# Pointwise convolution of six blocks as three products of rounded parts, in a one-core streaming encoder layer

## What is computed

```python
u = cv * jax.nn.sigmoid(cgl)
c = depthwise_conv(concat([conv_hist, u]), conv_w) + conv_b      # 31 taps, 256 channels
c = jax.nn.silu(layernorm(c, ln_g, ln_b)) @ w_pw + b_pw          # pointwise: 256 x 256
y_conv = c * jax.nn.silu(cg)
y = concat([y_attn, y_gla, y_conv]) @ w_out
return x + y
```

## Time and profile before

| | us |
|---|---|
| median of 3 runs | 925.39 (924.95 to 925.93) |
| the profiled execution, its own time | 925.71 |
| its span in the trace | 923.9 |
| PE busy | 890.1 (96%) |
| DVE busy | 784.4 (85%) |
| ACT busy | 481.6 (52%) |
| POOL busy | 215.7 (23%) |

### The profile page before, as it was taken

The page is one execution under the profiler, slowest core; times in us unless marked ns, Lnnn a source line. Parts: engine busy times, 40 slices in busy tenths (PEclk is TensorE's granted clock), DMA queues, the critical chain, the costliest instruction groups (busy, mean ns, idle before and its releaser), DMA issues. The chain is left out here.

```text
span 923.9 us, 15888 instructions
## 1 busy us (share of the span) xinstructions
PE 890.1 (96%) x5655; PEld 800.9 (87%) x5655; DVE 784.4 (85%) x1896; ACT 481.6 (52%) x1182; POOL 215.7 (23%) x259
## 2 busy tenths in 40 slices
PE   6889999999999999998999999999999999999997
PEld 5778888888888888876898888889999899998985
DVE  7898888888888888889879999888788969788994
ACT  7787666666676766668663261341515124142231
POOL 1432222222222222223022231311202012120310
PEclk9999999999999999999999999999999999999999
DMA  9553323222333333135451221121130312204021
GB/s 303 190 191 115 103 82 115 96 110 84 111 106 111 114 115 103 70 120 145 119 160 52 76 69 64 52 81 57 38 101 1 100 39 69 70 3 135 1 81 60
DMA packets 58062, 88.04 MB, mean 95 GB/s; under 512 B 10080, under 2 KB 34528, under 8 KB 57984
## 3 DMA queue, kind: packets, MB, share of 16 engines
q1 hardware_dynamic: 57984, 87.03, 28.8%
HBM read 60.47 MB, written 26.60 MB: 94 GB/s over the span
## 5 line engine op out<-in xcount | busy, mean ns | idle before, releaser
L1826 DVE SCALAR_TENSOR_TENSOR acc<-ub,cwh,acc 128x256 f32<-128x256 f32 (+1 forms) x480 | 230.4, 540 | 1.5 <-ACT acc L1323 0.7
L779 PE MATMUL J<-whi,xhi 128*128 128x512 f32 (+1 forms) x400 | 147.1, 368 | 7.4 <-DVE wlo L489 7.4
L2228 PE MATMUL J<-xbh,whi 128*128 128x256 f32 (+1 forms) x512 | 151.7, 296 | 0.3
L2228 PE MATMUL J<-xbl,whi 128*128 128x256 f32 (+1 forms) x512 | 146.2, 288 | 2.0 <-DVE xbl L587 2.0
L2228 PE MATMUL J<-xbh,wlo 128*128 128x256 f32 (+1 forms) x512 | 147.1, 287 | 0.0
L779 PE MATMUL J<-wlo,xhi 128*128 128x512 f32 (+1 forms) x400 | 143.1, 358 | 0.0
L779 PE MATMUL J<-whi,xlo 128*128 128x512 f32 (+1 forms) x384 | 136.3, 358 | 0.0
L2228 PEld LDWEIGHTS J<-xbh,whi 128*128 128x128 f32 x512 | 98.4, 192 | 2.6 <-DVE wlo L489 1.1
L2228 PEld LDWEIGHTS J<-xbl,whi 128*128 128x128 f32 x512 | 98.2, 192 | 2.2 <-issue 2.2
L2228 PEld LDWEIGHTS J<-xbh,wlo 128*128 128x128 f32 x512 | 98.5, 192 | 0.5
L779 PEld LDWEIGHTS J<-whi,xhi 128*128 128x128 f32 x400 | 76.9, 192 | 16.6 <-issue 7.4
(11 more groups left out here) (287 smaller groups left out, 2233.4 us busy)
## 6 DMA issues: line engine op xcount, KB each, us to landing
out<-res SPq DMA_DIRECT2D x60, 256.0 KB, 2.0
x_normed_scratch<-xraw SPq DMA_DIRECT2D x17, 512.0 KB, 2.9
xtok<-in_x_prompt SPq DMA_DIRECT2D x16, 512.0 KB, 3.6
res<-in_x_prompt SPq DMA_DIRECT2D x16, 512.0 KB, 4.5
xraw<-xT SPq DMA_DIRECT2D x15, 512.0 KB, 3.6
xbraw<-x_normed_scratch SPq DMA_DIRECT2D x14, 512.0 KB, 5.3
res<-out SPq DMA_DIRECT2D x14, 512.0 KB, 3.9
wraw<-in_w_in SPq DMA_DIRECT2D x52, 128.0 KB, 2.5
```

The lines of the kernel that those rows point to most:

```text
L779: last = nc.tensor.matmul(bank[:, 0:width], x[x_slot(ps, t)][:, k, :], w, start=(k == 0 and n == 0), stop=(k == KT - 1 and n == len(produc ...
L1826: nc.vector.scalar_tensor_tensor(acc[:, j, 0:frames], src, w, acc[:, j, 0:frames], ALU.mult, ALU.add).then_inc(conv_step, 1)
L2228: last = nc.tensor.matmul(bank[:, 0:w], wt, x[:, k, 0:w], start=(k == 0 and m == 0), stop=(k == KT - 1 and m == 2))
```

## The change

For groups 2 to 7 (blocks 1 to 6, whose pointwise step runs inside blocks 2 to 7) `pointwise` makes three products of rounded parts in place of the plain float32 product: 12 matmuls in place of 4. The weights `wpw` are split once (`wpw_split_hi` on ACT at the end of block 1, `wpw_split_lo` on DVE in block 2). For each group ACT rounds the SiLU result (`conv_gate_hi`, into the place of `cl`) and DVE makes the remainder (`conv_gate_lo`, in place of `cth`). The blocks 1 to 7 lay their x slices out 256 wide instead of 320, and the split weights lie in the 512 columns that this leaves free behind `xbh` and `xbl`; the tiles keep their sizes. Groups 0, 1 and 8 stay in plain float32.

```diff
-        xbh = sb("xbh", [P, KT, WIDE], F32R)
+        xbh = sb("xbh", [P, KT * WIDE], F32R)
...
+        ec = ExitStack()
+        cs_parts = [sb(f"cs_part{i}", [P, CJ, WIDE], F32R, ec) for i in range(2)]
+        ec.close()
         cl = sb("cl", [P, CJ, WIDE])
         cth = sb("cth", [P, CJ, WIDE])
+        wpw_hi, wpw_lo = [t[:, KT * 256:KT * 256 + CJ * CD] for t in (xbh, xbl)]
...
+        def by_tile(t, b):
+
+            return t[:, 0:KT * width(b)].rearrange("p (k n) -> p k n", n=width(b))
+
+        def rounded(g):
+
+            return 1 < g[0] < END
...
-            nc.scalar.activation(xbh[:, :, cols], raw_pair(b)[:, :, cols], ACT.Copy).then_inc(xb_hi, 1)
+            nc.scalar.activation(by_tile(xbh, b)[:, :, cols], raw_pair(b)[:, :, cols], ACT.Copy).then_inc(xb_hi, 1)
...
+            def wpw_split_hi():
+
+                act.wait_ge(slot_done, last_of_x(0) + 1)
+                act.wait_ge(consts_b, N_CONSTS_B)
+                nc.scalar.activation(wpw_hi, wpw_cols, ACT.Copy).then_inc(cs_hi, 1)
+
+            def conv_gate_hi(g):
+                gi, off, w, own = g
+                act.wait_ge(cs_ready, gi + 1)
+                nc.scalar.activation(cs_parts[0][:, :, off:off + w], cth[:, :, off:off + w], ACT.Copy).then_inc(cs_hi, 1)
...
                 take_gate(b, 1)
+                conv_gate_hi(done[0])
                 log_decay(b)
...
+            def wpw_split_lo():
+
+                dve.wait_ge(cs_hi, 1)
+                dve.wait_ge(slot_done, last_of_x(0) + 1)
+                nc.vector.tensor_tensor(wpw_lo, wpw_cols, f(wpw_hi), ALU.subtract).then_inc(cs_lo, 1)
+
+            def conv_gate_lo(g):
+                gi, off, w, own = g
+                dve.wait_ge(cs_ready, gi + 1)
+                dve.wait_ge(cs_hi, gi)
+                nc.vector.tensor_tensor(cs_parts[1][:, :, off:off + w], cth[:, :, off:off + w],
+                                        f(cs_parts[0][:, :, off:off + w]), ALU.subtract).then_inc(cs_lo, 1)
...
                         glu(b, 1)
+                        wpw_split_lo()
                         y_gla(g)
...
                     taps(2)
+                    conv_gate_lo(g)
                     logit_parts(b)
...
+                if rounded(g):
+                    pe.wait_ge(cs_lo, 1)
+                    pe.wait_ge(cs_hi, gi)
+                    for j in range(CJ):
+                        for n, (w_part, x) in enumerate(((wpw_hi, cs_parts[0]), (wpw_lo, cs_parts[0]), (wpw_hi, cs_parts[1]))):
+                            if n == 2:
+                                pe.wait_ge(cs_lo, gi)
+                            for k in range(CJ):
+                                last = nc.tensor.matmul(T[2][:, j * 256:j * 256 + w], wpw_part(w_part, k, j),
+                                                        x[:, k, off:off + w], start=(n == 0 and k == 0),
+                                                        stop=(n == 2 and k == CJ - 1))
+                    last.then_inc(pw_psum, 1)
+                    return
```

More of the change, by code:

```diff
@@ L278, in build @@
         ea.close()
-        xbh = sb("xbh", [P, KT, WIDE], F32R)
+        xbh = sb("xbh", [P, KT * WIDE], F32R)
         eb = ExitStack()
-        xbraw = sb("xbraw", [P, KT, WIDE], F32, eb)
-        res_end = [xbraw[:, :, :].rearrange("p k n -> p (k n)")[:, i * D:(i + 1) * D] for i in range(2)]
+        xbraw = sb("xbraw", [P, KT * WIDE], F32, eb)
+        res_end = [xbraw[:, i * D:(i + 1) * D] for i in range(2)]
         eb.close()
-        xbl = sb("xbl", [P, KT, WIDE], F32R)
+        xbl = sb("xbl", [P, KT * WIDE], F32R)
         th = sb("th", [P, 3 * P])
@@ L338, in build @@
         wpw = part("wpw").rearrange("p (j n) -> p j n", n=CD)
+        wpw_cols = part("wpw")
         convw = part("convw").rearrange("p (j n) -> p j n", n=CW)
@@ L423, in build @@
                                                     sem("conv_normed"))
+        cs_hi, cs_lo = sem("cs_hi"), sem("cs_lo")
         cnT_psum, cl_ready, cth_ready, cs_ready = (sem("cnT_psum"), sem("ln_affine_ready"), sem("conv_tanh"),
@@ L566, in raw_pair, with wpw_part @@
         def raw_pair(b):
-            return xb1raw if b == 1 else xbraw
+            return xb1raw if b == 1 else by_tile(xbraw, b)
         def pair_cols(b, i):
             return slice(i * P, i * P + (DEC if i == 2 else P))
+        def wpw_part(w, k, j):
+            return w[:, (CJ * k + j) * P:(CJ * k + j + 1) * P]
+        def by_tile(t, b):
+            return t[:, 0:KT * width(b)].rearrange("p (k n) -> p k n", n=width(b))
+        def rounded(g):
+            return 1 < g[0] < END
         def split_pair_hi(b, i):
@@ L586, in split_pair_lo @@
             cols = pair_cols(b, i)
-            nc.vector.tensor_tensor(xbl[:, :, cols], raw_pair(b)[:, :, cols], f(xbh[:, :, cols]), ALU.subtract).then_inc(
+            nc.vector.tensor_tensor(by_tile(xbl, b)[:, :, cols], raw_pair(b)[:, :, cols], f(by_tile(xbh, b)[:, :, cols]), ALU.subtract).then_inc(
                 xb_lo, 1)
@@ L592, in split_pair_lo_too @@
             cols = pair_cols(b, i)
[L593 removed]
+            nc.gpsimd.tensor_tensor(by_tile(xbl, b)[:, :, cols], raw_pair(b)[:, :, cols], f(by_tile(xbh, b)[:, :, cols]), ALU.subtract).then_inc(
                 xb_lo, 1)
@@ L1492, in _ @@
                         split_pair_hi(2, 1)
+                        wpw_split_hi()
                     continue
@@ L2208, in project_b @@
                 w = width(b)
+                xh, xl = by_tile(xbh, b), by_tile(xbl, b)
                 c, at = {"cgl": (0, 0), "cv": (0, 256), "gg": (2, 0), "cg": (2, 256), "gq": (3, 0), "gk": (3, P)}[kind]
@@ L2224, in project_b @@
                     hi, lo = weights(col, P)
-                    wt, x = ((hi, xbh), (lo, xbh), (hi, xbl))[m]
+                    wt, x = ((hi, xh), (lo, xh), (hi, xl))[m]
                     if first and (k, m) == (0, 2):
@@ L2387, in project_v @@
                     hi, lo = weights(KT * B.widths[0] + k * B.widths[1], B.widths[1])
-                    for m, (x, wt) in enumerate(((xbh, hi), (xbh, lo), (xbl, hi))):
+                    for m, (x, wt) in enumerate(((xh, hi), (xh, lo), (xl, hi))):
                         last = nc.tensor.matmul(bank[:, 0:B.widths[1]], x[:, k, at:at + P], wt, start=(k == 0 and m == 0),
```

## The result

| | kernel before | changed kernel |
|---|---|---|
| median, us (14 executions each) | 925.64 (924.74 to 926.56) | 927.48 (925.87 to 928.80) |
| ratio, 95% interval | | 1.0019 (1.0012 to 1.0026) |
| profiled execution, us (span) | 925.71 (923.9) | 927.36 (925.6) |
| mean granted clock | 0.994 | 0.993 |

The change made the kernel slower by 1.8 us. That is more than the forecast of 925.5 us and 0.3 us above the top of its range.

A forecast was written before the change was run, and what follows sets the result against it. PE was taken to bound the kernel from block 2 to block 6, with DVE leading at two places around that stretch. Terms −1.45 + 0.61 + 1.0 = +0.16 us on the median 925.39 gave 925.5 us, range 924.3 to 927.2.

The forecast's parts named there:

- The gain on PE: New pointwise product, 12 matmuls: 1.64 us in place of 1.97, saving 0.33 us a block (0.29 to 0.37).
- The layout: Wider x layout in blocks 1 to 7: costs nothing on PE.
- `wpw_split_lo`: Subtraction on DVE in block 2 ahead of the taps PE waits for: 0.61 us lost (0.55 to 0.75).
- `conv_gate_lo` in block 2: Subtraction on DVE: nothing leads from DVE in blocks 2 to 5, so its delay ends in idle time.
- the fall: Behind the longer wait before `conv_T` of block 2: clock at half for 3.41 us, costing 1.7 us; rival, chance 0.18.
- `conv_gate_lo` in block 6: DVE 1.24 us late, with 1.04 left to cover it at `q_full`: 0.2 us of the gain lost.
- `conv_gate_lo` in block 7: Subtraction held up by POOL, PE stalls 1.3 us at the fifth new matmul: block loses 1.0 us (0.5 to 1.1).
- the likeliest case itself: Whole kernel, both DVE costs landing and no clock fall: 925.5 us, 924.6 to 926.1; chance 0.60.
- The sum without it: Whole kernel, gains and costs without a clock fall: −1.45 + 0.61 + 1.0 = +0.16 us.

The follow-up runs named there:

- e7: Changed kernel with groups 2 to 6 rounded, group 7 plain, `wpw_split_lo` behind block 1's last taps, `conv_gate_lo` behind `logit_parts`: 923.89 us, ratio 0.9984.
- e5: Kernel before with only the wider layout of x, all products plain, no weight split: 925.25 against 925.29 us, ratio 1.0000.
- e9: Changed kernel, no edit, a single profiled execution, without a clock fall in block 2: 925.37 us.
- e3: Changed kernel with the product of block 7 (group 7) left in plain float32, without its rounding and subtraction: 925.56 us, ratio 0.9999.
- e2: Kernel before plus one useless 128x512 subtraction on VectorE ahead of `y_gla` in block 2: 927.07 us, ratio 1.0017.
- e13: Kernel before plus two useless 128x512 subtractions ahead of `y_gla` in block 2, the second waiting for the first: 927.50 against 925.44 us, ratio 1.0023.
- e1: Changed kernel with `wpw_split_lo` moved in block 2 behind the last taps and layer-norm statistics: 925.65 against 925.34 us, ratio 1.0005.
- e4: Changed kernel with `wpw_split_lo` moved behind the taps in block 2 and group 7 left in plain float32: 924.49 us, ratio 0.9989.
- e8: Changed kernel, no edit, a single profiled execution, with a clock fall in block 2: 928.40 us.
- e12: Kernel before plus one useless subtraction ahead of `y_gla` in block 2, a single profiled execution without a clock fall there: 924.88 us.
- e10: Kernel before plus one useless subtraction ahead of `y_gla` in block 2, a single profiled execution with a clock fall there: 927.41 us.

## Why the prediction was wrong

**The gain on PE: right.** I took 1.64 us for the new product in place of 1.97, and the rows show 1.65. A block gained 0.29 us (0.25 to 0.29) and not 0.33; summed over block 3 the new matmuls and those next to them save 0.33, and 0.05 us comes back at the first matmuls of the output projection, in a gap too short to be listed as a wait. e7, whose VectorE is not late there, has the whole 0.33. The Trainium skill's 109 ns a matmul ("TensorE: Matmul & The Clock Gate", "Back-to-back issue gap") didn't come about either: the twelve take 1.41 us, 0.118 each.

**The layout: right**, by e5.

**`wpw_split_lo`: right.** Forecast +0.61 us and a wait of 2.27, found +0.61 and 2.27.

**`conv_gate_lo` in block 2: missed.** I had written that in blocks 2 to 5 nothing leads from VectorE and its delay ends in idle time. For block 2 that is wrong: without the fall PE loses 0.35 us to the late `ybc` (e9; e3 has the same), so block 2 gains nothing. With the fall this is hidden. In blocks 3 to 5 it is the 0.05 us above, at the same place.

**`conv_gate_lo` in block 6: right in kind.** VectorE ran late, its idle time at `q_full` was used up, and PE lost 0.11 us where I had 0.2. The subtraction ended where I had it, 0.54 us behind the end of POOL's product (818.08 to 818.82), but not for my reason: it had begun only at 818.62, when ACT's rounding was done, and took 0.74 us, near its ordinary 0.69.

**`conv_gate_lo` in block 7: right.** Forecast 1.0 us lost and a stall of 1.3 at the fifth matmul; found 1.12 and 1.18. The subtraction ended 0.55 us behind POOL's product, as the earlier trace rows had it. The Trainium skill's rule on who excludes whom ("SBUF — State Buffer", "Who interferes with whom") agrees, with POOL first.

**The step that failed is the likeliest case itself:** that the granted clock stays full behind the longer wait. I named the fall as a rival, with its place and its price, and gave it 0.18. The sum without it was +0.16 us by my terms and is +0.75 by the trace without a fall (e9); the measured difference is 1.8 us (1.1 to 2.4). So of the 1.6 us by which I was off, some 0.6 lie in terms of the sum (0.35 in block 2, the rest mostly 0.05 a block on PE) and 1.05 are left for the fall. At 1.2 us net a fall, that is a fall in some nine of ten executions; with the interval it is between three and all of ten. Three other kernels with a lengthened wait (e2, e3, e13) exceed the sum of their steps by 0.95, 0.3 and 0.8 us, a quarter to two thirds of a fall, and of these only the excess of e2 is clear of zero by its own interval. The traces have a fall in four of eight, and the mean clocks point to 0.6 of one. All together say that the rival happens in about half of the executions or more, and not in 0.18 of them; the share itself stays rough. The rows in hand spoke for it more than I let them: the one wait of that length that I had read, 2.12 us, was followed by a fall, and the one of 1.66 was not. I treated it as a mishap with a small chance, where the only two rows there were put it near even.

**The range** went to 927.2, which is the forecast and one fall, with none of the spread that I allowed for elsewhere (the kernel before was itself 0.25 us higher in this measurement than in the one that I started from). Price of the fall: 1.7 forecast, 1.51 found. At half clock the matmuls of 272 columns come 0.227 us apart and not twice 0.126, which would be 0.252, so less is lost than half of the stretch: 3.41 × (1 − 0.126/0.227) = 1.5.

What stays open: what decides whether a given execution falls. The length of the wait alone does not, since the same wait goes both ways, and doubling the added work did not measurably raise the excess. That the fall makes up the excess of the timed executions is worked out from profiled ones and fits their mean clocks; no timed execution shows it at its place.

## What to carry to other kernels

Work added on the engine that PE waits for costs more than its own length when it makes a wait of PE longer: here 0.61 us of VectorE cost 1.6 us (0.7 to 2.4), and a fall of the clock in some of the executions is what the traces offer for the rest. So price such a wait with the fall in it, as soon as the trace holds a wait of similar length with one behind it, and let the forecast be a mixture. And the same twelve matmuls are worth it or not by where their operands are made: with two short instructions moved and one block left out, e7 is 1.4 us faster than the kernel before, while the change as it was written is 1.8 slower.

## What was not expected of the hardware

A wait of the same length is followed by a half clock in one execution and not in the next. Ahead of the transposes of block 1 PE waits 2.10 to 2.13 us in every trace, and the clock fell behind it in 9 of 14 profiled executions (not in e1, e4, e7, e8, e12).

What a fall costs depends on the engine that leads behind it. In block 2, where PE leads, it is 1.51 us, which stay to the end in e10; in the changed kernel 0.35 of them cover the wait for `ybc`. In block 1, where VectorE leads behind it, e12 has no fall and the kernel before has one: matched as above, e12 is ahead by 1.41 us at 471.55 and by 1.56 at 539.13, so the fall cost 0.15. Early in pass A it is 1.0: matched between 60 and 90 us, the six traces with no half clock near 70 us (after, e4, e5, e9, e12, e13) gain 0.99 to 1.04 us on the kernel before, which has one there, and the seven others at most 0.18. The count of falls in a trace, or the mean clock, thus says little of the time: e8 and e9, the same kernel and 3.0 us apart, both have a mean clock of 0.996.
